# Six homes instead of four for the split weight chunks of a mixture-of-experts stage

## The reference, cut to what matters

```python
logits = xt @ router_w + router_b;  top_val, top_idx = lax.top_k(logits, TOP_K)
gate = softmax(top_val)
...
hh  = xblk @ w1[e] + b1[e]                    # 1024 -> 2048, "up"
glu = minimum(hh[:, :D_FF], 7.0); lin = clip(hh[:, D_FF:], -7.0, 7.0)
act = glu * sigmoid(1.702 * glu) * (lin + 1.0)
y   = act @ w2[e] + b2[e]                     # 1024 -> 1024, "down"
out[token] += gate * y
```

## Time and profile before

| | |
|---|---|
| median of 3 runs | 2221.84 us (2213.68 to 2222.48) |
| the profiled execution, its own time | 2221.01 us |
| its span, first to last instruction | 2219.2 us |
| TensorE busy | 2132.5 us, 96% |
| VectorE busy | 1734.6 us, 78% |
| ScalarE busy | 1273.8 us, 57% |
| read from HBM | 528.97 MB |

### The profile page before, as it was taken

How to read it: one execution, slowest core, us unless ns; L and a number is a source line. 1 busy time by engine, 2 the same in 40 slices (tenths; PEclk the granted TensorE clock), 3 DMA queues, 4 the chain that set the end, 5 groups by cost and what they waited for, 6 DMA issues and landing times.

```text
span 2219.2 us, 29496 instructions
## 1 busy us (share of the span) xinstructions
PE 2132.5 (96%) x10033; PEld 1683.0 (76%) x10033; DVE 1734.6 (78%) x1668; ACT 1273.8 (57%) x1265; POOL 788.0 (36%) x293
## 2 busy tenths in 40 slices
PE   7999999999999999999999999999999999999996
PEld 3888888888887888788777777777777777777764
DVE  6756655655636866856879999999999999999996
ACT  6413222132223723732467888788888787888784
POOL 3000000000202023000614655657655557656575
PEclk9999999999999999999999999999999999999998
DMA  9322223132231021045689999999999999999994
GB/s 308 124 95 95 95 77 140 55 129 76 77 132 39 1 95 57 1 151 213 222 320 385 398 396 401 389 400 396 401 399 396 391 390 396 392 391 387 375 398 169
DMA packets 132755, 541.06 MB, mean 244 GB/s; under 512 B 13779, under 2 KB 22115, under 8 KB 98622
## 3 DMA queue, kind: packets, MB, share of 16 engines
q1 hardware_dynamic: 123336, 516.43, 60.6%
q0 software_dynamic: 9040, 19.30, 3.5%
q10 hardware_dynamic: 296, 4.21, 0.5%
HBM read 528.97 MB, written 19.82 MB: 247 GB/s over the span
## 4 chain that ended last, share of the span: by engine, by line
PE 74%; DVE 9%; DMA 7%; issue 6%; ACT 3%; POOL 1%; DVEq 0%; ACTq 0%; SPq 0%; POOLq 0%
PE ps L2423 70%; DMA raw<-in_exp_w 3%; DVE wlo L2168 3%; DVE hlo L2168 2%; DMA ar<-in_exp_w 2%; ACT hhi L1362 2%; PE ps L2770 1%; DMA ar<-h_d,ar 1%; DVE ylo L2320 1%; PE ps L2990 1%; DVE ar L2343 1%; POOL list_d L883 1%; PE ps L3005 1%; DMA ar<-in_ctx 0%; ACT hlo L1413 0%
## 5 line engine op out<-in xcount | busy, mean ns | idle before, releaser
L962 POOL DMA_INDIRECT out_x<-ar,cur x32 | 388.2, 12132 | 250.5 <-DVE ar L2343 189.8
L2423 PE MATMUL ps<-whi,yhi 128*128 128x512 f32 x800 | 293.9, 410 | 30.6 <-DVE wlo L2168 30.3
L2168 DVE TENSOR_TENSOR hlo<-raw,hhi 128x2048 fp32r<-128x2048 f32 x132 | 298.5, 2281 | 23.8 <-ACT hhi L1362 23.8
L2168 DVE TENSOR_TENSOR wlo<-raw,whi 128x2048 fp32r<-128x2048 f32 x132 | 296.9, 2277 | 0.2 <-ACT whi L1362 0.2
L1362 ACT ACTIVATE hhi<-raw 128x2048 fp32r<-128x2048 f32 x132 | 252.8, 1917 | 52.8 <-PE ps L2423 38.4
L828 POOL TENSOR_SCALAR sm<-ss 128x8 f32<-128x8 f32 (+3 forms) x39 | 13.2, 338 | 754.9 <-ACT ar L1185 487.6
L2423 PE MATMUL ps<-hhi,yhi 128*128 128x512 f32 x800 | 278.7, 394 | 0.1
L1362 ACT ACTIVATE whi<-raw 128x2048 fp32r<-128x2048 f32 x132 | 249.1, 1918 | 37.7 <-PE ps L2423 36.8
L1529 DVE TENSOR_TENSOR wlo<-raw,whi 128x2048 fp32r<-128x2048 f32 x56 | 128.2, 2289 | 159.4 <-ACT whi L1024 159.4
L2423 PE MATMUL ps<-whi,hhi 128*128 128x512 f32 x592 | 233.3, 394 | 0.0
L2423 PE MATMUL ps<-whi,hlo 128*128 128x512 f32 x592 | 230.8, 390 | 0.0
(11 more groups left out here) (378 smaller groups left out, 4517.5 us busy)
## 6 DMA issues: line engine op xcount, KB each, us to landing
raw<-in_exp_w SPq DMA_DIRECT2D x264, 1024.0 KB, 8.3
ar<-in_exp_w SPq DMA_DIRECT2D x132, 1024.0 KB, 9.0
raw<-in_w_in SPq DMA_DIRECT2D x44, 1024.0 KB, 5.0
raw<-in_w_mod SPq DMA_DIRECT2D x22, 1024.0 KB, 6.8
raw<-in_w_br_ret SPq DMA_DIRECT2D x8, 1024.0 KB, 5.2
ar<-in_x SPq DMA_DIRECT2D x8, 512.0 KB, 7.8
raw<-in_w_br_diff SPq DMA_DIRECT2D x4, 1024.0 KB, 5.0
raw<-in_w_out SPq DMA_DIRECT2D x4, 1024.0 KB, 9.6
```

The lines of the kernel that those rows point to most:

```text
L962: pool.indirect_dma_start(a["out"], bass.IndirectOffsetOnAxis(ap=rows, axis=0), F(A_Y, D)[0:m], None, bounds_check=L - 1, oob_is_err=False ...
L2168: V.tensor_tensor(e_wlo[j % ESPL], e_raw[s], e_whi[j % ESPL].bitcast(F32), ALU.subtract).then_inc(e_lo, 1)
L2423: return pe.matmul(out, lhsT, rhs, start=start, stop=stop, skip_group_check=skip)
```

## The change

There are six homes for the high and six for the low parts, the home of a chunk has the number of its raw slot, and `hi_e` waits for `e_used` of chunk c-6. The two new pairs of homes lie in the arena: in the dead rows of x_new and the biases' place and, for the last, in the routing tables. So chunk 4 of item 0 waits for the rows to be stored, chunk 5 for the biases and for the list's scatters; the SiLU's result moves to 14848, where the wide list was, and the wide list to a table of constants that is no longer read. The orders change: three (not two) low parts stand before `act_low`, two more between it and the output product; `act_high` stands after the high of chunk 4; the high of 11 stands ahead of the SiLU and of `lower_up`; the product of the gate stands behind one low part more; `write_sel` and `write_sel2` stand later; `fold_y` stands after chunk 2 and not after chunk 1. Nothing is computed otherwise.

```diff
-ESPL = 4
+ESPL = 6
+TURNED_AT, GIVE_AT = 5, 7
...
-A_XG, A_Y, A_GS, A_TH, A_AC = 0, 1024, 2048, 3072, 9216
+A_XG, A_Y, A_GS, A_TH, A_AC = 0, 1024, 14848, 3072, 9216
+A_SPLIT = (A_XN, A_BSRC), (A_XN + 2048, A_RT)
...
-        list_wide = F(A_PICK + 2 * SLOTS_H * N_EXPERTS, N_EXPERTS, 2).bitcast(I32)
+        list_wide = cst[:, C_WIN:C_WIN + 2 * N_EXPERTS].rearrange("p (e w) -> p e w", w=2).bitcast(I32)
...
                 if isinstance(i, int) and i == 0 and j < ESPL:
                     act.wait_ge(tile_done, DONE_OUT + 2 * LT)
+                    if j == KH:
+                        act.wait_ge(n2_done, LT)
+                        act.wait_ge(stored, 16 * LT)
+                    if j == KH + 1:
+                        act.wait_ge(bias_lo, 2)
                 else:
                     act.wait_ge(e_used, chunk(i, j) - ESPL + 1)
...
-                act.activation(e_whi[j % ESPL], e_raw[s], ACT.Copy).then_inc(e_hi, 1)
+                act.activation(e_whi[s], e_raw[s], ACT.Copy).then_inc(e_hi, 1)
...
             def item(i, half_b, half_a, half, half_n, n=None):      # ScalarE
-                for j in range(AHEAD, ESPL):
+                for j in range(AHEAD, TURNED_AT):
                     hi_e(i, j)
-                if not (isinstance(i, int) and i == 1):
-                    write_sel2(i - 1)
                 if half_b:
                     lower_y(i - 2)
                 act_high(i - 1, half_a)
-                for j in range(ESPL, MOE_N - 1):
+                if not (isinstance(i, int) and i == 1):
+                    write_sel2(i - 1)
+                for j in range(TURNED_AT, MOE_N):
                     hi_e(i, j)
-                write_sel(i + 1)
                 if half:
                     lower_up(i)
-                    hi_e(i, MOE_N - 1)
                     x_high(i + 1, half_n)
+                    hi_e(i + 1, 0)
                     glu_half(n)
                 else:
                     glu(i)
-                    hi_e(i, MOE_N - 1)
+                    hi_e(i + 1, 0)
                     x_high(i + 1, half_n)
-                for j in range(AHEAD):
-                    hi_e(i + 1, j)
+                write_sel(i + 1)
+                hi_e(i + 1, 1)
...
+            act.wait_ge(gathered, 32)
+            act.wait_ge(cur_ready, 1)
             glu(0)
...
             def item(i, half_b, half_a, half, half_n, buf_b, n=None, n_b=None):      # VectorE
-                for j in range(AHEAD, ESPL):
+                for j in range(AHEAD, TURNED_AT):
                     lo_e(i, j)
                 act_low(i - 1, half_a)
+                for j in range(TURNED_AT, GIVE_AT):
+                    lo_e(i, j)
                 if half_b:
                     give_half(i - 2, n_b, buf_b)
                 elif not isinstance(i, int) or i > 1:
                     give_y(i - 2, chunk(i - 1, MOE_N - 1), buf_b)
-                for j in range(ESPL, MOE_N - 1):
+                for j in range(GIVE_AT, MOE_N):
                     lo_e(i, j)
                 if half:
-                    lo_e(i, MOE_N - 1)
                     x_low(i + 1, half_n)
-                    activate_half(i, n, lambda: lo_e(i + 1, 0))
+                    lo_e(i + 1, 0)
+                    activate_half(i, n, lambda: lo_e(i + 1, 1))
+                else:
+                    activate(i, lambda: lo_e(i + 1, 0))
+                    x_low(i + 1, half_n)
                     lo_e(i + 1, 1)
-                else:
-                    activate(i, lambda: lo_e(i, MOE_N - 1))
-                    x_low(i + 1, half_n)
-                    for j in range(AHEAD):
-                        lo_e(i + 1, j)
...
-                    if half_b and kk == 1:
+                    if half_b and kk == 2:
                         fold_y(n_b)
```

More of the change, by code:

```diff
@@ L290, in build @@
         k_ctx = nc.alloc_sbuf_tensor_at("k_ctx", [P, 2, C], F32R, offset=ar_at + 4 * (A_TMP + 2 * L))
+        e_more = [[nc.alloc_sbuf_tensor_at(f"e_more{w}{k}", [P, KH, COL], F32R, offset=ar_at + 4 * A_SPLIT[w][k])
+                   for k in range(2)] for w in range(2)]
         ct = sb("ct", [P, 2, KC])
@@ L504, in build @@
         e_raw = [flat(v) for v in e_raw]
-        e_whi = [flat(v) for v in (whi[:, 0, :, :], whi[:, 1, :, :], hh[0][:, 0], hh[0][:, 1])]
-        e_wlo = [flat(v) for v in (wlo[:, 0, :, :], wlo[:, 1, :, :], hh[1][:, 0], hh[1][:, 1])]
+        e_whi = [flat(v) for v in (whi[:, 0, :, :], whi[:, 1, :, :], hh[0][:, 0], hh[0][:, 1], *(m[:, :, :] for m in e_more[0]))]
+        e_wlo = [flat(v) for v in (wlo[:, 0, :, :], wlo[:, 1, :, :], hh[1][:, 0], hh[1][:, 1], *(m[:, :, :] for m in e_more[1]))]
         mhi = [yhi[:, c, :] if c < KH else hhi[:, c, 0:L] for c in range(KC)]
@@ L1479, in _ @@
             act.activation(bias2, b2, ACT.Copy).then_inc(b2_hi, 1)
-            for j in range(ESPL, FIRST):
+            for j in range(KH, FIRST):
                 hi_e(0, j)
@@ L1483, in _ @@
                 hi_e(1, j)
-            act.activation(junk32[:, 0:1], ones[:, 0:1], ACT.Silu)
+            act.activation(nmx[:, 0, 0:1], ones[:, 0:1], ACT.Silu)
+            act.wait_ge(gathered, 32)
+            act.wait_ge(cur_ready, 1)
             glu(0)
@@ L2167, in lo_e @@
                 dve.wait_ge(e_loaded[s], rounds(i, j) * 16 + 16)
-                V.tensor_tensor(e_wlo[j % ESPL], e_raw[s], e_whi[j % ESPL].bitcast(F32),
+                if isinstance(i, int) and i == 0 and j == KH + 1:
+                    dve.wait_ge(listed, 16 * LT * TOP_K)
+                V.tensor_tensor(e_wlo[s], e_raw[s], e_whi[s].bitcast(F32),
                                 ALU.subtract).then_inc(e_lo, 1)
@@ L2407, in last_low @@
                 give_half(end - 1, end, None)
-                for j in range(AHEAD, ESPL):
+                for j in range(AHEAD, MOE_N - FIRST):
                     lo_e(end + 1, j)
@@ L3027, in up @@
                         cols = slice(b * COL, (b + 1) * COL)
-                        wh, wl = e_whi[kk % ESPL][:, cols], e_wlo[kk % ESPL][:, cols]
+                        wh, wl = e_whi[raw_slot(i, kk)][:, cols], e_wlo[raw_slot(i, kk)][:, cols]
                         mm(o, xthi[:, kk, :], wh, kk == 0, False)
@@ L3041, in up, with down_chunk @@
                         between(kk)
-            def down_chunk(j, kk, o, c, half):
+            def down_chunk(s, kk, o, c, half):
                 q = kk % 2
                 cols = slice(q * D + c * COL, q * D + (c + 1) * COL)
-                wh, wl = e_whi[j % ESPL][:, cols], e_wlo[j % ESPL][:, cols]
+                wh, wl = e_whi[s][:, cols], e_wlo[s][:, cols]
                 mm(o, acthi[:, kk, :], wh, kk == 0, False)
@@ L3065, in down @@
                         for c in range(2):
-                            last = down_chunk(j, 2 * k + q, ps[:, 6 + c, :], c, half)
+                            last = down_chunk(raw_slot(at_i, j), 2 * k + q, ps[:, 6 + c, :], c, half)
                     last.then_inc(e_used, 1)
@@ L3154, in last_down @@
                     for q in range(2):
-                        last = down_chunk(k, 2 * k + q, ps[:, 2 + c, :], c, True)
+                        last = down_chunk(raw_slot(end + 1, k), 2 * k + q, ps[:, 2 + c, :], c, True)
                     if k == MOE_N - FIRST - 1:
```

## The result

The changed kernel is slower: 2251.77 us, the median of 4 runs (2239.98 to 2256.36), against 2218.2 of the kernel before in runs beside it (4 runs, 2213.68 to 2222.48). The ratio is 1.0141, interval 1.0113 to 1.0169. The forecast was 2199 with a range up to 2222, so the time lies outside it, on the side that the text gave 0.12. The profiled execution took 2256.36 us.

What follows compares the result with a forecast made beforehand. VectorE, TensorE and the DMA engines stand within 4% of the beat, holding each other through four homes. A pair: 63.85 + 0.5 + 0.85 = 65.2 against 66.56; 14 x 1.36 = 19, plus 3 at the start: 2199 us, range 2181 to 2222.

Steps and rivals of the forecast that it cites:

- it just fits: nothing in the sum: GpSimd: six VectorE openings in a pair suffice for its eight instructions, as a copy and a scatter can share one.
- The rival: GpSimd becomes late, gathers miss the opening at `act_low`: 2 to 3 us a pair net, 2232 to 2256; chance 0.14.
- VectorE's waits, 2.71 us a pair: Expert stage: six homes and the high of 11 placed earlier remove VectorE's gaps, 66.56 - 63.85 us a pair.
- in front of one kind of home alone: Profile before: ScalarE waits 90.5 us over 950 us for TensorE to free a home, of one kind only.
- Late landings, 0.85 us: Weight transfers in the expert stage: loads landing late cost 0.85 us a pair, which is 407 GB/s.
- the first rival: The transfers are the bound already: a pair at 401 GB/s takes 66.1 us, 2214 up to 2221; chance 0.2.
- ScalarE's chain: ScalarE's steps before the copy of chunk 0: VectorE waits 0.5 us in the half item, nothing in the wide.
- VectorE's floor, 63.85: Expert stage: VectorE's busy time, 63.85 us a pair, is unchanged by any edit.
- The later product, TensorE's slack and not the beat: Gate product one low part later: TensorE waits some 1.5 us, without lengthening the pair unless a transfer is late.
- The start, 3 us: Items 0 and 1: earlier splitting of chunks makes VectorE up to 4.4 us readier for item 2; 3 taken.
- last 19: Profile before, expert stage: in the last 19 of 40 slices the core moves 375 to 401 GB/s.
- The loop of the later product: From product through TensorE and VectorE to the next half item's product: 64.2 us, just above VectorE's floor.

Runs made afterwards that it cites:

- the first experiment: The changed kernel with GpSimd's copy of indices for the next gather moved ahead of the scatter: 2207.26 us, ratio 0.9916 to the kernel before.
- mended: With GpSimd's index copy moved ahead of the scatter; the mended kernel is the changed kernel with this edit, 2207.26 us.
- orders alone: The changed kernel with four homes and not six, the new orders kept on all engines: 2240.76 us, ratio 1.007.
- homes alone: The changed kernel with its six homes, but the orders of before on all engines: 2281.55 us, ratio 1.0276.
- homes alone, mended: Six homes with the orders of before, and GpSimd's index copy moved ahead of the scatter: 2213.98 us, ratio 0.997.

## Why the prediction was wrong, step by step

- *GpSimd, "it just fits: nothing in the sum".* This is the step that failed. I counted openings and instructions. What counts is the time between them: the copy and the gather behind it need two openings, and 0.86 us passes from the end of the one to the request of the other, so that an opening of 1.2 us is over by 0.2 us after the request. The openings at `act_low` and at the output product of the wide item let no gather in here. What the runs showed in place of "it just fits": gathers of 26.11 us and more, and 57.2 us of TensorE waiting for rows. The rival had it right, and the point from which it decides too: the copy isn't done before the clamp. Its figures were 52 us for the rows and 42 for TensorE; measured are 49.9 and 45.3. Its price of 2 to 3 us a pair is measured at 2.2, and 2251.77 lies in its 2232 to 2256. It had the gather wait for the next clamp, though, and the gather ended 2.6 us ahead of it. Its chance of 0.14 was too low: the pair at 1366.78 already showed scatter, copy and gather held up one behind the other, and its being the shortest pair only said that the rows weren't late yet.
- *"VectorE's waits, 2.71 us a pair", to be won by six homes and the new place of chunk 11.* The waits for `whi` (18.5 to 3.8 us) and TensorE's for a low part went, as forecast. ScalarE's waits for a home became waits for loads only where the rows come in time: in the first experiment 9.2 + 4.8 + 0.7 us for homes are left of 140.4. (That they stood "in front of one kind of home alone" was a misreading: 90.5 us stand in front of one kind and 49.9 in front of the other.) But VectorE's waits were GpSimd's openings; the copy moved ahead of the scatter shows that both can be had. And they weren't worth 2.71 us: the six homes by themselves took nothing off a pair (66.7 us, mended), and with the new orders it is 0.4.
- *Late landings, 0.85 us.* Mis-sized. The mended pair is 66.1 to 66.2 at 396 GB/s, which is the price of the first rival and 2.3 us above VectorE's floor. Of that rival the cause holds for the mended kernel only, not for the kernel before. I took 407 GB/s as nearer to the pair rows, and it wasn't: the 417 of a short window are not sustained. The forecast of 2199 wouldn't have been met without the loss either; 2203 to 2207 would have been its time, inside the range of 2188 to 2209, with 7.8 us of the gain at the start where 3 were counted.
- *ScalarE's chain.* Half item: 0.5 taken, 1.10 measured. Wide item: "nothing" taken, 1.77 measured; its SiLU waits for TensorE (3.5 us at the longest) with the copy of chunk 0 behind it, which I hadn't counted. Neither is in the time, since the landings are behind them: removing the 1.77 gave 1.4 us of 2207, less than the spread of the runs (2205.55 to 2212.14).
- *VectorE's floor, 63.85.* Right: 64.11 where the bytes are fewer.
- *The later product, TensorE's slack and not the beat.* Right with six homes: waits of 1.0 us (9.1 in 9) and 2.5 us of 2206 for putting it back. With four homes it costs (orders alone).
- *The start, 3 us ("up to 4.4").* Too small: TensorE's `turn_x` in item 1 stands 7.8 us earlier with homes alone and 7.7 in the mended kernel (1207.71 for 1215.36). In the changed kernel it would be the same, but TensorE waits there 7.68 us for the first rows, and the start is lost.
- *Slips that change nothing.* The last of the "last 19" slices stands at 169 GB/s, not at 375 or more. The loop of the later product adds up to 24 + 39.6 + 0.3 = 63.9 us, not 64.2.

The best version here is the last with all bytes: index copy ahead of the scatter, copy of chunk 0 ahead of the SiLU, product right behind the clamp. It takes 2203.39 us, 0.75% less than before and 2.1% less than the changed kernel.

Open: what it is that lets a gather in. In the changed kernel `act_low` (two instructions in 0.74 us, each with a PSUM input and one from SBUF) did not, and with a clamp of 0.67 us (PSUM alone) in its middle it did. Length alone is no answer: the output product of 1.27 us let none in, and in the kernel with the copy of chunk 0 first a gap of 0.24 us did (a gather of 1.46 us from 1702.36, the gap from 1702.96). The kind of operands alone is none either: with orders alone an `act_low` of 0.75 us at 2147.16 let in a gather that ended at 2148.10. So the openings counted here tell where a gather can get in, not where it will.

## What to carry to other kernels

Before closing an engine's gaps ask who works in them: here a helper engine with some 6 us of work of its own in a pair (two scatters of 1.6, two gathers of 1.0, four copies of 0.2) lived on VectorE's waits, and no share of busy time tells it, since held-up time counts as busy (788 us before, 847 after); its own timeline, with one pair that has a gap beside one that has none, does. Of dependent steps on a held-up engine count the chain from request to opening, and take every step out of it that can be done earlier. Run each half of a change alone: here it took homes alone, mended, to see that the homes won the start, and that only homes and orders together shorten a pair. And a resource within 1% of the one that binds takes the whole rest of the gain, so price it by the longest rows, not by the best short one.

## What the runs showed of the hardware

GpSimd's instructions, indirect DMAs and copies of 64x2 alike, are held up while VectorE runs two-input subtractions in SBUF back to back: an index copy takes 0.2 us and up to 26.25 (in the kernel with the copy of chunk 0 first), a gather 0.98 to 30.92 (in the first experiment). Most of those read here end in or shortly behind a gap of VectorE or another instruction of it; the gathers of 26.11 us in the changed kernel end in the middle of a subtraction. Once let in, an indirect DMA runs on beside subtractions: VectorE is idle for 0.76 us ahead of its low part at 1516.65, and the scatter of 1501.39 ends at 1517.26, 0.61 us into it. The Trainium skill, page SBUF — State Buffer, section Who interferes with whom, infers that descriptor generation is spared by such a `tensor_tensor`. These rows neither prove nor refute it: the DMAs are held up as a whole, up to 30.92 us, but what is left behind the opening runs on. Which of their steps is held no run parts, and "not held up at all", as the prediction took it, is what the rows contradict.

Where the transfers bind, loads of 1 MB with a gather and a scatter in each item hold 396 GB/s on this core over 780 us. The Trainium skill, page DMA: Bandwidth & Descriptors, section Bandwidth, has 425 GB/s for a single core with one large transfer; no window read here came to it; the highest is the 417 over 12 us of the earlier trace rows. The DMA share in the windows says nothing on this: over 780 us it is 1.01 where transfers bind, 1.01 with fewer bytes, where VectorE is full, and 1.00 in the kernel before with fewer bytes.
